# Weight sums of one projection formed earlier, and a new order of the mixer's column pairs

## What is computed

```python
a = rmsnorm(x, g_mix);  u = a @ w_in          # q, k, v, gates, og, B, C, h
h = mlstm(q, k, v, ig, fg)                    # 4 heads, chunks of tokens, carried state
h_m = sigmoid(og) * headnorm(h)               # columns 0..511 of the mixer's result
y_c = B * causal_conv3(C * h)                 # columns 512..1023
x = x + concat(h_m, y_c) @ w_out
f = rmsnorm(x, g_ffn)
x = x + (silu(f @ w_gate) * (f @ w_up)) @ w_down
e = rmsnorm(pe @ w_ple, g_ple)
x = x + sigmoid(x @ w_pg) * e                 # the last projection
y = rmsnorm(x, g_final)
```

## Time and profile before

| | us |
|---|---|
| median of three runs | 2703.61 (2699.7 to 2706.51) |
| the profiled execution, its own time | 2702.62 |
| its span | 2700.8 |
| PE busy (mean granted clock 0.972) | 2514.3 |
| DVE / ACT / POOL busy | 1492.5 / 952.2 / 1137.0 |
| DMA read and written | 347.44 and 106.35 MB |

### The profile page before, as it was taken

How to read it: one execution, slowest core, us unless ns; L and a number is a source line. 1 busy time by engine, 2 the same in 40 slices (tenths; PEclk the granted TensorE clock), 3 DMA queues, 4 the chain that set the end, 5 groups by cost and what they waited for, 6 DMA issues and landing times.

```text
span 2700.8 us, 41211 instructions
## 1 busy us (share of the span) xinstructions
PE 2514.3 (93%) x15882; PEld 2452.3 (91%) x15882; DVE 1492.5 (55%) x2288; ACT 952.2 (35%) x1766; POOL 1137.0 (42%) x939
## 2 busy tenths in 40 slices
PE   4999788999999879999999999998998999999997
PEld 3899788999999878999999999998898989999997
DVE  4666787764455684447753333467456664333355
ACT  4344443333333534334422222244233442222233
POOL 3566655665555443333332333324423333323333
PEclk7999898999999899999999999999999999999998
DMA  5445534544455545566455445575555545654444
GB/s 167 162 148 201 178 119 149 179 180 167 150 183 179 188 144 181 162 188 201 154 182 165 144 148 172 167 219 168 173 164 188 181 159 172 190 176 151 159 141 159
DMA packets 306309, 456.46 MB, mean 169 GB/s; under 512 B 21683, under 2 KB 218596, under 8 KB 305606
## 3 DMA queue, kind: packets, MB, share of 16 engines
q1 hardware_dynamic: 239014, 269.13, 30.2%
q10 hardware_dynamic: 67104, 184.70, 21.5%
HBM read 347.44 MB, written 106.35 MB: 168 GB/s over the span
## 4 chain that ended last, share of the span: by engine, by line
PE 48%; DVE 5%; issue 2%; DMA 1%; ACT 1%; POOL 1%; DVEq 0%; POOLq 0%; SPq 0%; ACTq 0%
PE bank L504 15%; PE bank L506 15%; PE bank L505 15%; DMA wring<-weight_parts 1%; DVE qlo L1561 1%; DVE ess L2142 0%; PE bank L603 0%; DVE sg L2270 0%; PE bank L666 0%; PE bank L614 0%; PE bank L669 0%; DVE R L1720 0%; PE bank L672 0%; DMA wraw<-w_out 0%; POOL wring L2412 0%
## 5 line engine op out<-in xcount | busy, mean ns | idle before, releaser
L2412 POOL TENSOR_TENSOR wring<-wraw,wring 128x512 fp32r<-128x512 f32 x612 | 874.6, 1435 | 1282.4 <-ACT wring L1121 1278.3
L504 PE MATMUL bank<-qhi,wring 128*128 128x352 f32 (+1 forms) x3588 | 1180.1, 329 | 115.1 <-issue 23.3
L506 PE MATMUL bank<-qhi,wring 128*128 128x352 f32 (+1 forms) x3588 | 1162.5, 324 | 0.0
L505 PE MATMUL bank<-qlo,wring 128*128 128x352 f32 (+1 forms) x3588 | 1161.9, 324 | 0.0
L504 PEld LDWEIGHTS bank<-qhi,wring 128*128 128x128 f32 x3588 | 689.4, 192 | 139.8 <-issue 130.6
L1121 ACT ACTIVATE wring<-wraw 128x512 fp32r<-128x512 f32 x612 | 382.5, 628 | 878.9 <-PE bank L506 731.8
L505 PEld LDWEIGHTS bank<-qlo,wring 128*128 128x128 f32 x3588 | 689.1, 192 | 0.0
L506 PEld LDWEIGHTS bank<-qhi,wring 128*128 128x128 f32 x3588 | 686.6, 191 | 0.0
L504 PE MATMUL bank<-hid,wring 128*128 128x352 f32 (+1 forms) x1056 | 340.7, 323 | 14.0 <-DVE wide L2229 7.1
L506 PE MATMUL bank<-hid,wring 128*128 128x352 f32 (+1 forms) x1056 | 339.3, 321 | 0.0
L505 PE MATMUL bank<-hid,wring 128*128 128x352 f32 (+1 forms) x1056 | 338.5, 321 | 0.0
(11 more groups left out here) (302 smaller groups left out, 2436.5 us busy)
## 6 DMA issues: line engine op xcount, KB each, us to landing
wring<-weight_parts ACTq DMA_DIRECT2D x336, 512.0 KB, 4.2
weight_parts<-wring SPq DMA_DIRECT2D x168, 512.0 KB, 3.1
wraw<-w_down SPq DMA_DIRECT2D x33, 1024.0 KB, 6.7
wraw<-w_in SPq DMA_DIRECT2D x27, 512.0 KB, 4.7
wraw<-w_in SPq DMA_DIRECT2D x12, 1024.0 KB, 6.3
wraw<-w_gate SPq DMA_DIRECT2D x11, 1024.0 KB, 5.8
wraw<-w_up SPq DMA_DIRECT2D x11, 1024.0 KB, 5.9
wraw<-w_gate SPq DMA_DIRECT2D x22, 512.0 KB, 4.2
```

The source lines that it names most:

```text
L504: nc.tensor.matmul(o, hi, mh, start=begins, stop=False, skip_group_check=True)
L505: nc.tensor.matmul(o, hi, ml, start=False, stop=False, skip_group_check=True)
L506: return nc.tensor.matmul(o, lo, mh, start=False, stop=ends, skip_group_check=True)
L2412: nc.gpsimd.tensor_tensor(wlo[e % RING][:, :].rearrange(v, k=k), w.src, whi[e % RING][:, :].rearrange(v, k=k), ALU.subtract).then_inc(lo_d ...
```

## The change

The four pairs of `pg` in part 0 load their sums from `weight_parts`, as parts 1 and 2 do. The 16 sums are formed, split and stored earlier in part 0, in groups p = 3, 5, 7, 9: SP loads the raw `w_pg` columns of one pair into a buffer of its own (`spare_raw`, 1 MB), and four spare entries are put into the ring behind the sixth and the eighth entry of the down group and behind the first and third of the up pair. PE passes over them. DVE sums in place. The store and load semaphores are six each instead of four.

The mixer's pairs come in the order q, k, v, v, C, H, o, C, H, o, B, B; the second convolution runs at m = 35 to 40 and the second sigmoid at m = 43. Heads are merged at m = 44 (block 0), 46 (block 1 up to the last chunk) and 52, in part 2 53, (the last chunk), where T1 follows at once. The high part of operand 0 is at m = 50, its low part at 51; those of operand 4 one and two after the last merge.

```diff
+SPARE_PAIRS = (3, 5, 7, 9) if SPARE else ()
+SPARE_SUMS = ("S1", "S3", "S2", "S4")
...
-IN_COLS = [0, 256, 512, 768, COL_C, COL_H, COL_O, COL_B, COL_C + 256, COL_H + 256, COL_O + 256, COL_B + 256]
-IN_KINDS = ["q", "k", "v", "v"] + ["C", "H", "o", "B"] * 2
+IN_COLS = [0, 256, 512, 768, COL_C, COL_H, COL_O, COL_C + 256, COL_H + 256, COL_O + 256, COL_B, COL_B + 256]
+IN_KINDS = ["q", "k", "v", "v", "C", "H", "o", "C", "H", "o", "B", "B"]
+IN_HALF = [0, 0, 0, 0, 0, 0, 0, 1, 1, 1, 0, 1]
...
+        self.last_heads = 53 if self.sample else 52
...
+    spare_raw = at("spare_raw", [P, 2048], F32, w0 + 20480 + RING * 4096 + 5632)
...
+    def add_spare(r, n):
+        pair_, m = n // 4, n % 4
+        at_ = by_quarters(spare_raw)
+        name = SPARE_SUMS[m]
+        add_entry(r, at_[{"S1": "A22", "S3": "A21", "S2": "A11", "S4": "A12"}[name]], n + 1)
+        entries[-1].spare = n
+        keep_entry(("pg", pair_), name)
+        spare_last[pair_] = n_prepared[0]
...
-        if q and CACHED:
+        stored = CACHED and (q or of[0][0] == "pg" and SPARE)
+        if stored:
...
+            n = 4 * SPARE_PAIRS.index(p) if p in SPARE_PAIRS and not q.n else None
+            add_pair(q.n, "gate", p, w_gate_v, 256 * p)
             if down_before(p) is not None:
-                add_down(down_before(p))
-            add_pair(q.n, w_up_v, 256 * p, product_order("up", p))
+                add_down(down_before(p), n)
+            add_pair(q.n, "up", p, w_up_v, 256 * p, None if n is None else {0: n + 2, 2: n + 3})
...
+            def spare_weights(i):
+                if i:
+                    sp.wait_ge(lo_done, spare_last[i - 1])
+                else:
+                    sp.wait_ge(*written[("e", 0)])
+                sp.dma_start(spare_raw[:, :].rearrange("p (k n) -> p k n", k=KC), w_pg_v[:, :, 256 * i:256 * i + 256])\
+                    .then_inc(spare_in, 16)
...
+                    if SPARE and q.n == 0 and r in (24, 30, 36, 42):
+                        spare_weights((r - 24) // 6)
...
                 if e >= RING:
-                    act.wait_ge(prod, entry_end[e - RING])
+                    if entries[e - RING].spare is None:
+                        act.wait_ge(prod, entry_end[e - RING])
...
+            def ahead():
+                one_ahead()
+                if n_hi[0] < len(entries) and entries[n_hi[0]].spare is not None:
+                    one_ahead()
...
-                    if m in (22, 50):
-                        i = 6 if m == 22 else 10
+                    if m in (22, 43):
+                        i = 6 if m == 22 else 9
...
-                    if m == 28:
+                    if m == 20:
                         act.wait_ge(conv_made, 2 * q.n + 1)
...
-                    if m == 53:
+                    if m == 50:
                         high_of(q, "out", 0)
-                    if m == 54:
+                    if m == q.last_heads + 1:
                         high_of(q, "out", 4)
...
+            def spare_sum(n):
+                i, m, v = n // 4, n % 4, by_quarters(spare_raw)
+                name = SPARE_SUMS[m]
+                if m == 0:
+                    dve.wait_ge(spare_in, 16 * (i + 1))
+                else:
+                    dve.wait_ge(spare_sums, n)
+                out, a, b, op = {"S1": ("A22", "A21", "A22", add), "S3": ("A21", "A11", "A21", sub),
+                                 "S2": ("A11", "A22", "A11", sub), "S4": ("A12", "A12", "A11", sub)}[name]
+                nc.vector.tensor_tensor(v[out], v[a], v[b], op).then_inc(spare_sums, 1)
...
-                    if m >= 0 and m % 28 in range(14, 20):
-                        convolve(q, m // 28, (m % 28 - 14) // 3, (m % 28 - 14) % 3)
-                    if m == 52:
-                        merge(q, 0).then_inc(src_ready, 1)
-                    if m == 53:
-                        link(merge(q, 1))
+                    if m in range(14, 20) or m in range(35, 41):
+                        convolve(q, m // 35, (m % 35 - (0 if m >= 35 else 14)) // 3, (m % 35 - (0 if m >= 35 else 14)) % 3)
+                    u, c, last = q.U, q.blocks, q.chunks[-1]
+                    if m == 44:
+                        merge(q, c[0], 2).then_inc(src_ready, 1)
+                    if m == 46:
+                        link(merge(q, slice(c[1].start, q.tiles[last][0]), last - 1))
+                    if m == 51:
+                        low_of(q, "out", 0)
+                    if m == q.last_heads:
+                        link(merge(q, slice(q.tiles[last][0], q.T), last))
                         made(q, "out", 0)
-                        u, c = q.U, q.blocks
                         nc.vector.tensor_tensor(u[:, 0:4, c[1]], u[:, 0:4, c[1]], u[:, 0:4, c[0]], sub).then_inc(src_ready, 1)
-                    if m == 54:
-                        low_of(q, "out", 0)
+                    if m == q.last_heads + 2:
+                        low_of(q, "out", 4)
...
-                low_of(q, "out", 4)
                 dve.wait_ge(gated, 6 * q.n + 6)
```

More of the change, by code:

```diff
@@ L335, in add_plain @@
             add_entry(r, v[:, k, n], 0, j == 0)
+            if spares and j in spares:
+                add_spare(r, spares[j])
         end[r] = n_prepared[0]
@@ L367, in add_down @@
             add_plain(w_down_v[:, 4 * g - 2:4 * g + 2, 512 * a:512 * a + 512], 4, 512,
-                      [(ALL4, slice(P * n, P * n + P)) for n in range(4)])
+                      [(ALL4, slice(P * j, P * j + P)) for j in range(4)], {1: n, 3: n + 1} if a and n is not None else None)
     for q in supers:
         for i in range(IN_PAIRS):
-            add_pair(q.n, w_in_v, IN_COLS[i], product_order("in", i))
+            add_pair(q.n, "in", i, w_in_v, IN_COLS[i])
             if i == 0:
@@ L487, in multiplied, with skip_spares @@
                 written[key], drained[key] = (prod, n_prod[0]), (free[b], n_free[b])
+            def skip_spares():
+                while n_entry[0] < len(entries) and entries[n_entry[0]].spare is not None:
+                    n_entry[0] += 1
             def entry_ready(e):
@@ L493, in entry_ready @@
                 else:
-                    pe.wait_ge(parts_loaded[w.loaded % 4], 16 * w.loads)
+                    pe.wait_ge(parts_loaded[w.loads % 6], 16 * ((w.loads + 5) // 6))
             def operand_ready(q, st, i):
@@ L852, in down @@
             def down(q, g):
-                e, ks = n_entry[0], 4 if g else 2
+                n, ks = 8 if g else 4, 4 if g else 2
+                es = [e for e in range(n_entry[0], n_entry[0] + n + 4) if entries[e].spare is None][0:n]
                 xs_ = range(4) if g else (2, 3)
@@ L1097, in link, with one_ahead @@
                 act.wait_ge(act_own, n_own[0])
-            def ahead():
+            def one_ahead():
                 e = n_hi[0]
@@ L1531, in copy_at, with one_ahead @@
                 return nc.vector.tensor_scalar(out, in_, 1.0, None, mul)
-            def ahead():
+            def spare_sum(n):
[8 more added lines that the diff above has]
+                nc.vector.tensor_tensor(v[out], v[a], v[b], op).then_inc(spare_sums, 1)
+            def one_ahead():
                 e = n_sum[0]
                 n_sum[0] += 1
+                if e < len(entries) and entries[e].spare is not None:
+                    spare_sum(entries[e].spare)
                 for name, r, v, where, turn, first, second in sums_at.get(e, ()):
@@ L1557, in ahead @@
                         nc.vector.tensor_tensor(v["A11"], v["A12"], second[:, :, :], sub).then_inc(sums, 1)
+            def ahead():
+                one_ahead()
+                if n_sum[0] < len(entries) and entries[n_sum[0]].spare is not None:
+                    one_ahead()
             def low_of(q, st, i):
@@ L2413, in ahead @@
                                         ALU.subtract).then_inc(lo_done, 1)
+            def ahead():
+                one_ahead()
+                if n_lo[0] < len(entries) and entries[n_lo[0]].spare is not None:
+                    one_ahead()
             def low_of(q, st):
```

107 lines of the change are left out of this document (62 added, 45 removed).

## The result

The changed kernel takes 2670.09 us (median of 4 runs, 2667.16 to 2674.94) against 2701.9 (4 runs, 2699.7 to 2706.51) for the kernel before, beside which it ran: ratio 0.9882, 95% interval [0.9859, 0.9904]. It is 31.8 us faster, where 44 were forecast. 2670 lies in the range of 2645 to 2682, but the gains of the sum were all put too large. The profiled execution took 2672.54, its span is 2670.8.

What follows compares the result with a forecast made beforehand. PE, busy 93% of the span, was taken to bound the kernel. Moved sums -23.1 and mixer order -21.0 gave -44.1 against 2702.62: 2658.5, plus half of 1.0, so 2659 us; range 2645 to 2682.

Steps and rivals of the forecast that it cites:

- Rival 1: Part 0's `pg` stays bound by DVE, so 6.9 us stay: 2666 us; chance 0.10.
- Rival 2: Mixer pairs at m = 35 and 42: DVE falls behind, PE waits 2 to 4 us per part: 2671; chance 0.14.
- part B: The mixer's new order in all three parts: -7.5 - 5.5 - 8.0 = -21.0 us, bounds -27 and -9.
- Sums of `pg`: Part 0's `pg` becomes part 1's, 21.9 us less, and down(5) 2.2 less: together -24.1 us.
- The groups: Groups p = 3, 5, 7, 9 take the spares' work at +0.25 us each: +1.0, bounds 0 and +7.0.
- rival 3: DVE and POOL block each other in the groups, delaying P7's PSUM read and the next gate pair: +9, 2668; chance 0.08.
- Rival 4: Spares' buffers wait for copy, subtraction and store, and PE pays at all 16: 80 us lost, 2738; chance 0.03.
- Part 0's seam: Mixer to `out`: DVE's stream 4.5 us shorter, `w_out` load issued 4.0 us earlier: -8.5 us.
- Part 1: Seam from mixer to `out`: the 4.47 us wait goes and the lower-clock stretch gives back 1.7: -6.2 us.
- Part 2: Seam from mixer to `out`: the 6.76 us wait goes and the lower clock gives back 2.3: -9.1 us.
- What the order adds: Mixer pairs: moved convolution and merges cost +1.0, +0.7, +1.1 us in parts 0, 1, 2; bounds 0 and +4 each.
- slack of about 1 us: Part 2's seam: last head slice still at m = 53, its T1 one product later; slack shrinks to about 1 us.

Runs made afterwards that it cites:

- experiment 6: Changed kernel, but in part 0's duos the second member's first sum is asked for one DVE call later; 2667.94 us, ratio 0.9883 to the kernel before.
- experiment 7: Changed kernel, but in part 2 ACT copies the last head slice out at m = 52, ahead of the split awaiting `w_out`; 2670.09 us, ratio 0.9882.
- spares_down: Changed kernel with all four spare entries of a group in the down group, none in the up pair; 2666.25 us, ratio 0.9873.
- one_in_up: Changed kernel with three spare entries of a group in the down stretch and one in up, behind its first entry; 2666.39 us, ratio 0.9873.

## Why the prediction was right, and where its sum was not

The direction, the two causes and the range held; the sum overstated the gain by 14 us of span. The range was wider than its own working: the bounds of the parts add up to 2652 and not 2645, rivals 1 and 2 to 2678 and not 2682, and part B's bounds of -27 and -9 are more than its terms give (-25.4 and -11.8). 2670 lies within the narrower ends as well. Step by step:

- **Sums of `pg`, -24.1.** Measured -22.05, and 21.5 to 22.9 less in the ten kernels that have the moved sums. The mechanism is the one forecast: DVE 50.6 of 70.75 us, clock 0.98. What was too much is that part 0's `pg` would be part 1's: it stays 2.3 us longer than part 1's 68.5. PE's waits there add up to 7.3 us against 5.6 (1.01 of it is one wait for the next part's x tile, which part 1 doesn't have), and its last 3.0 us run at the lower clock, in part 1 the last 1.7, which is worth 0.7. Rival 1 (6.9 us stay) falls.
- **The groups, +1.0.** The term mis-sized most against its own size. The groups that hold the spares are at 175.66 us to the hundredth, as argued. The price is paid in the pair behind them, 1.05 us four times (measured +4.1). That is rival 3's mechanism, the next gate pair put off through DVE and POOL, but once in a group and at 1.05 instead of 1.3 us. The working put the spares' work into the down stretch, with POOL some 6 us busier there; it was 2.1 us busier, the fourth subtraction came in the up pair (818.94), and POOL's backlog was not followed into the next pair. Rival 4 falls: no row of the group waits for a store.
- **Part 0's seam, -8.5.** Two terms. DVE's stream from the load to P7 was to lose 4.5 us of work: its busy time went from 37.11 to 32.56, 4.55 less, but it is now idle for 1.75 us of it (1.19 waiting for POOL, 0.29 for PE), so the stretch went from 37.34 to 34.31. The other 4.0 us were wrong: the load was said to wait for ACT's split behind the sigmoid. The sigmoid left, and the load was issued 0.30 us later and used 0.56 us later, counted from the stage's start. The rows of experiment 6 show why: the load hangs on POOL's subtractions, which ran without a gap in the kernel before too. In the new order ACT's first split of that chain even starts 0.3 us later in the stage, behind DVE's merge (1.77 us) and sum.
- **Part 1, -6.2.** The 4.47 us wait and the 1.7 us of clock went as forecast, and low part 4 came at 1194.17, 7.0 us after P7's end, as worked out. 1.82 us of waiting came for something that the working left out: the prepared weights of P5, whose load ACT issues behind high part 4. Its rows stand below this list.
- **Part 2, -9.1.** 6.76 and 2.1 to 2.3 of clock went, 3.50 us of waits came. ACT stands 4.74 us before the `w_out` load with the last head slice behind it, so low part 4 ended at 2063.02, 0.10 us before P5's start; the "slack of about 1 us" didn't count that. Once it was early (experiment 7), a weight load was late here as well. A further 1.0 us is in how waits are read: PE loses some 0.25 us more at each than the bracket says (the start at 2063.12 lies 2.00 us behind the one before it and 0.23 before the next, where the pace of these matmuls is 0.153), and there are now four waits and one of 0.10 where there was one.
- **What the order adds, +2.8.** Nothing: the fifth to eleventh pairs are 0.55 us shorter in all. Rival 2 falls; in the second o pair no wait shows in parts 0 and 1, and part 2 has one of 1.80 us in the tenth pair with an eleventh pair 1.18 us shorter.
- **The rule of the skill.** The forecast had cited the Trainium skill (SBUF — State Buffer, "SBUF: two separate sides") for the moved sums: a DVE instruction with two SBUF inputs and a GpSimd one that reads SBUF keep each other out for a whole instruction. The trace agrees, and in the way in which it cost time: the second low part of the hidden layer, with two SBUF inputs, takes 0.88 us in a gap of POOL and 1.98 within a subtraction. It hit an instruction that the change doesn't touch.

The load behind part 1's 1.82 us, on ACT's queue, and what SP issues beside it:

```profile
1191.19 1.01 ACTq L1171 DMA_DIRECT2D wring<-weight_parts  x2
...
1191.12 0.35 SPq L1117 DMA_DIRECT2D wide<-stored_x  x1
```

Both wait for T1 and go out at once. PE goes on at 1198.79, 7.6 us after the weight load was issued, where the median of these loads is 4.2 us to landing. In the kernel before a weight load went out beside this reload of x as well (at 1215.71) and took 8.2 us, but was in time. So two things make the 1.82 us, ACT's late issue and a load some 3.3 us slower than the median beside the reload; no run takes them apart.

Not settled: whether part 1's wait would go with the weight loads issued ahead of high part 4, or with the reload of x issued behind them. Neither was tried.

## What to carry to other kernels

When the time of a load is to be moved, find the last of the engines that free its buffer, not the first one that looks busy: here ACT had a sigmoid in front of the split, but POOL behind it ran without a gap. When work is put beside a stage with room, follow each engine's backlog past the stage's end: the bill came one pair later. And when a wait on one engine's result goes, read the in-order queues of the other engines at that place, with all that they issue behind a wait and what else is released by the same event, before calling it gone.

## What the runs showed of the hardware

DVE and POOL slow each other by whole instructions, and a mean hides it. Of the 69 low parts of the hidden layer (most 128x704 or 128x672) 38 took under 1.1 us in the kernel before, 29 took 1.5 to 2.1, two took longer, and none lay between 1.1 and 1.5. In the changed kernel it is 34 and 33: four more long ones, one for each gate pair that lost 1.05 us. In `spares_down` and `one_in_up` it is 38 and 29 again.

It goes both ways. POOL's run of five subtractions in part 0's tail took 7.54 us in the kernel before and 8.90 in the changed one. The first four took 6.29 and 6.28; the fifth took 1.29 and 2.66, beside DVE's low part of operand 0 (2.71 us there, 1.62 in part 1), which the new order puts at that place. For planning, POOL's subtraction took 1.3 us at the median and up to 1.75 in the groups; beside the low parts here it took 1.94 and 2.66.
